# Query strips a head ahead, an older head's sums inside the key strip, norm roots read from PSUM, and a later start of two weight loads

## The chip, the cores and the metric

The kernel runs on one core of a Trainium2 chip, alone. The metric is device time in microseconds of that core, the median of several executions.

## What is computed

Two two-layer blocks, one after the other, on 256 latent tokens and 256 context tokens with 2048 features, everything in float32. The first block has a gated linear recurrence (layer 0) and a differential attention with 16 heads (layer 1), the second two layers (2 and 3) that join a gated spatial unit of 8 groups with grouped-query attention of 8 query heads on 2 key-value heads. Every layer starts with a modulated RMS norm and ends in an output projection with a gate and a residual. Cut to what the change touches:

```
def diff_attn_mixer(...):            # layer 1, per head
    q, k = rms_norm(q), rms_norm(k), rotated
    attn = softmax(q0 k0) - lam * softmax(q1 k1)
    o = rms_norm(attn @ v, subln_g) * (1 - lam_init)
    return (o * silu(g)) @ w_out
def second_block(...):               # layers 2 and 3
    h = rms_norm_2(x, norm_w) * (1 + scale) + shift
    u, v_sgu, za, q, k, v, zb = split(h @ w_in)
    q = rope(rms_norm_2(q, q_norm_w));  k = rope(rms_norm_2(k, k_norm_w))
    attn = softmax(q k_all * HEAD_DIM ** -0.5) @ v_all
    y = concat([sgu * silu(za), attn * silu(zb)]) @ w_out
```

Layer 3 is the last one: its queries and gates are wanted for the 256 latent tokens alone, in layer 2 for all 512.

## The kernel before

Activations lie feature-major: 16 tiles of 128 features by 512 tokens. Float32 products are made on TensorE (PE) in three reduced-precision products: high weights by high activations, high by low, low by high. A **strip** is a weight block of 2048 rows by 128 columns, 1 MB, in two halves of eight 128 by 128 tiles. Each strip goes the same way: SyncE loads a half into `raw` (`load_strip`, L215) once VectorE (DVE) has split what lay there before; ScalarE (ACT) copies it to a rounded high part (`split_hi`, L223), DVE subtracts that to get the low part (`split_lo`, L231), and PE runs 48 matmuls (`strip`, L249 to L251). There are two strip buffers. A strip's buffer is free for the next but one when its matmuls are done, so both splits wait for `strip_done`; ACT and DVE call `next_strip` right after it.

The order of all work is written out by hand: each engine runs its own list (`start_*`, `lru_*`, `att_*`, `sgu_*`, `kv_*`, `gqa_*`, `out_*`, `norm_*`) and waits on counting semaphores. Per-head work is a software pipeline: `body(j, par)` handles iteration i, in which head i is `here`, head i-1 `before` and head i-2 `older`. An engine never passes a waiting instruction of its own list.

- **Opening** (`start_*`). Eight groups of modulation weights of 4 MB each (four loads of 1 MB, POOL L1807, one buffer of four slots) feed products on PE (L299). SyncE holds the loads of strips 2 and 3 back until the products of six groups are done.
- **Norms of layers 1 to 3.** PE spreads the inverse root to all partitions in PSUM bank 6 (L493), ACT copies it to SBUF (L503), and DVE uses it in two products for each of 16 feature tiles (L541, L543); ACT and DVE make high and low parts of the result (L522, L550), and PE's first strips (L288) follow tile by tile.
- **Layer 1, per head** (`att_*`): key strip, scores, the ones-product that sums the squares of the older head's output (`sso`), query strip, the ones-product for the key (`ssk`, L1114), value strip, transposes, gate strip, weighted values. On ACT the four exponentials (L1174) stand ahead of the older head's square root (L1178), with a switch of the function table between them.
- **Layers 2 and 3, per head** (`gqa_*`): query strip of head i, its rotation of head i-1 (L1603), transposes of head i-2's weights (L1610, L1614), gate strip of head i, the ones-product for head i's query norm (L1622), weighted values of head i-2 (L1631, L1634), scores of head i-1 (L1645, L1648). ACT splits first and then copies and squares the query (L1688, L1689), which gives `q_evac`. The gate's bank goes through a tanh on ACT (L1706). Behind the last head the first two output strips (`out_first`, L625, L262) are interleaved with what is left of the pipeline, while ACT and DVE turn the 16 tiles of the mixer's output into high and low parts (`to_high`, `to_low`, L604, L609).

Of the kernel before, what the change touches and what calls it, by code (L numbers as in the profile page):

```python
# [83 lines left out]
def build(nc, ins, out):  # L84
    with ExitStack() as ctx:
# [444 lines left out]
        def norm_dve(dve, l):  # L530
# [5 lines left out]
            dve.wait_ge(S["rstd_done"], l + 1)  # L536
            dve.wait_ge(S["strip_done"], layer_strip[l])

            def context(k, c):
                dve.wait_ge(S["h_ready"], KT * l + k - 3)  # L540
                dve.scalar_tensor_tensor(out=hs4[c][:, 0:T], in0=xl[:, k, :], scalar=mod_a[:, bass.ds(k, 1), 0],  # L541
                                         in1=nb["rstd"][:, 0:T], op0=ALU.mult, op1=ALU.mult)
                dve.scalar_tensor_tensor(out=hs4[c][:, T:NT], in0=y[:, 1, k, :], scalar=mod_a[:, bass.ds(k, 1), 1],  # L543
                                         in1=nb["rstd"][:, T:NT], op0=ALU.mult, op1=ALU.mult).then_inc(S["hf_done"], 1)
# [529 lines left out]
        def att_pe(pe):  # L1074
            def body(j, par):
# [3 lines left out]
                def chunk(n):  # L1079
                    return lambda half: mod_chunk(pe, M_ATT + j, 2 * par + n) if half else None  # L1080
                first = isinstance(i, int) and i == 0
# [4 lines left out]
                elif here:  # L1086
                    ge(pe, A["v_evac"], i)
                    strip(pe, att_strip(j, par, 0), psum[:, K_BANK, :], NT, chunk(0))
# [13 lines left out]
                if older:  # L1102
                    pe.wait_ge(A["o_evac"], i - 1)
                    pe.matmul(psum[:, M_BANK, 0:T], ones, osq, start=True, stop=True).then_inc(A["sso"], 1)
# [49 lines left out]
        def att_act(act):  # L1154
            def body(j, par):
# [3 lines left out]
                if last:  # L1159
                    to_high(act, 1, 0, 6)  # L1160
                if here:
# [14 lines left out]
                if older:  # L1176
                    act.wait_ge(A["sso"], i - 1)
                    act.activation(osq, psum[:, M_BANK, 0:T], ACT.Sqrt, scale=1.0 / P, bias=eps_col).then_inc(A["sdo"], 1)  # L1178
# [402 lines left out]
        def gqa_strip(lay, j, par, c):  # L1581
            return Strip(S_NET2 + lay * L2_STRIPS + L2_ATT, 2 * par + c, j, 4)

        def gqa_pe(pe, lay):
            base, wide_ = HEADS2 * lay, lay == 0
            n = NT if wide_ else T
            def body(j, par):
                i = 2 * j + par
                here, before, older = live(i, HEADS2), live(i - 1, HEADS2), live(i - 2, HEADS2)
                last, end = (isinstance(i, int) and i == HEADS2 + n for n in range(2))  # L1590
                if last:
                    pe.wait_ge(B["q_evac"], base + HEADS2)
                    pe.wait_ge(B["sz"], base + HEADS2)
                    out_first(pe, 2 + lay, 0, 4)
                if end:
                    out_first(pe, 2 + lay, 10, 14)
                if here:
                    ge(pe, B["q_evac"], base + i)
                    strip(pe, gqa_strip(lay, j, par, 0), psum[:, 0, 0:n], n)
                if before:  # L1600
                    pe.wait_ge(B["qn"], base + i)
                    ge(pe, B["qt1"], base + i - 1)
                    pe.matmul(psum[:, 5, 0:T], rot2, q2[:, 0:T], start=True, stop=True).then_inc(B["rotq"], 1)  # L1603
                if last:
                    out_first(pe, 2 + lay, 4, 8)
                if older:
                    pe.wait_ge(B["attn"], base + i - 1)
                    for qt in range(2):
                        for kt in range(4):
                            mm = pe.transpose(psum[:, 2 + qt, kt * P:(kt + 1) * P], p2[qt][:, kt * P:(kt + 1) * P], ident)  # L1610
                    if wide_:
                        for qt in range(2):
                            for kt in range(2):
                                mm = pe.transpose(psum[:, 4, kt * T + qt * P:kt * T + (qt + 1) * P],  # L1614
                                                  p2[2][:, qt * T + kt * P:qt * T + (kt + 1) * P], ident)
                    mm.then_inc(B["attn_t"], 1)
                if here:
                    ge(pe, B["sz"], base + i)
                    strip(pe, gqa_strip(lay, j, par, 1), psum[:, 1, 0:n], n)
                    pe.wait_ge(B["q_evac"], base + i + 1)  # L1620
                    ge(pe, B["sdq"], base + i)
                    pe.matmul(psum[:, 6, 0:n], ones, q2s[:, 0:n], start=True, stop=True).then_inc(B["ssq"], 1)  # L1622
                if last:
                    out_first(pe, 2 + lay, 8, 10)
                if end:
                    out_first(pe, 2 + lay, 14, OUT_REST)
                if older:
                    pe.wait_ge(B["attn_sb"], base + i - 1)
                    ge(pe, B["y2"], base + i - 2)
                    for kt in range(4):  # L1630
                        mm = pe.matmul(psum[:, 7, 0:T], v2[par][:, kt * P:(kt + 1) * P], at2[:, kt, :], start=(kt == 0), stop=(kt == 3))  # L1631
                    if wide_:
                        for kt in range(2):
                            mm = pe.matmul(psum[:, 7, T:NT], v2[par][:, T + kt * P:T + (kt + 1) * P], at2c[:, kt, :],  # L1634
                                           start=(kt == 0), stop=(kt == 1))
                    mm.then_inc(B["av"], 1)
                if before:
                    if isinstance(i, int) and i == 1:
                        pe.wait_ge(B["kr"], 2 * (lay + 1))
                        pe.wait_ge(B["v_sb"], 2 * (lay + 1))  # L1640
                    pe.wait_ge(B["qr"], base + i)
                    ge(pe, B["attn_sb"], base + i - 1)
                    keys = k2[1 - par]
                    for qt in range(2):
                        mm = pe.matmul(psum[:, 2 + qt, :], q2r[:, qt * P:(qt + 1) * P], keys, start=True, stop=True)  # L1645
                    if wide_:
                        for qt in range(2):
                            mm = pe.matmul(psum[:, 4, qt * T:(qt + 1) * T], q2r[:, T + qt * P:T + (qt + 1) * P], keys[:, T:NT],  # L1648
                                           start=True, stop=True)
                    mm.then_inc(B["scores"], 1)  # L1650
            rounds(pe, body, HEADS2, 2, 4)

        def gqa_act(act, lay):
            base, wide_ = HEADS2 * lay, lay == 0
            n = NT if wide_ else T

            def body(j, par):
                i = 2 * j + par
                here, before, older = live(i, HEADS2), live(i - 1, HEADS2), live(i - 2, HEADS2)
                last, end = (isinstance(i, int) and i == HEADS2 + n for n in range(2))  # L1660
                if before:
                    act.wait_ge(B["ssq"], base + i)
                    act.activation(q2s[:, 0:n], psum[:, 6, 0:n], ACT.Sqrt, scale=1.0 / P, bias=eps_col).then_inc(B["sdq"], 1)
                if last:
                    to_high(act, 2 + lay, 0, 4)
                if older:
                    act.wait_ge(B["negmax"], base + i - 1)
                    ge(act, B["attn_t"], base + i - 2)
                    for qt in range(2):
                        ins_ = act.activation(p2[qt], psum[:, 2 + qt, :], ACT.Exp, scale=SCALE2, bias=nm2[:, qt:qt + 1],  # L1670
                                              accum_out=rs2[:, qt:qt + 1])
                    if wide_:
                        for qt in range(2):
                            ins_ = act.activation(p2[2][:, qt * T:(qt + 1) * T], psum[:, 4, qt * T:(qt + 1) * T], ACT.Exp, scale=SCALE2,
                                                  bias=nm2[:, 2 + qt:3 + qt], accum_out=rs2[:, 2 + qt:3 + qt])
                    ins_.then_inc(B["expd"], 1)
                if last:
                    to_high(act, 2 + lay, 4, 8)
                if end:
                    to_high(act, 2 + lay, 14, OUT_REST)  # L1680
                if here:
                    st = gqa_strip(lay, j, par, 0)
# [3 lines left out]
                    if isinstance(i, int) and i == 0:  # L1686
# [3 lines left out]
                if older:  # L1690
# [488 lines left out]
```

## Time and profile before

| | us |
|---|---|
| median of 3 executions | 2798.53 (2798.18 to 2805.46) |
| the profiled execution | 2805.79 |
| its span, first to last instruction | 2804.1 |
| PE busy in the span | 2639.0 (94%) |
| DVE busy | 2045.8 (73%) |
| ACT busy | 1224.6 (44%) |
| mean granted TensorE clock | 0.977 |

The profiled execution took 1.7 us more than its span and 7.3 us more than the median. PE is busy nearly everywhere, so the time is told by where PE stands idle and by where its clock is at the lower level. A PE row gives the start of a group of matmuls and its busy time; the next group starts some tenths before the busy time is over, since matmuls overlap. The number in square brackets is the idle time of the engine just before, with what ended it.

### The profile page before, as it was taken

The numbers are of one execution on the slowest core, as the hardware profiler recorded it, in microseconds if no ns is written. First come the engines' busy times: TensorE is split into PE (matmuls) and PEld (weight loads), VectorE is DVE, ScalarE is ACT, GpSimd is POOL, SyncE is SP. The second block draws the span as 40 slices with busy tenths as digits, with TensorE's granted clock in tenths as the row PEclk, the third lists the DMA queues.
The fourth block names the chain that finished last, engine by engine and source line by source line (L and its number), as shares of the span: only waits on it lengthen the run. The fifth ranks groups of instructions, "written<-read, shape, count | busy, mean of one in ns | idle before, by whom it ended". The sixth has DMA issues, their size and how long they took to land.

```text
span 2804.1 us, 39539 instructions
## 1 busy us (share of the span) xinstructions
PE 2639.0 (94%) x13490; PEld 2133.3 (76%) x13490; DVE 2045.8 (73%) x3196; ACT 1224.6 (44%) x1875; POOL 211.6 (8%) x402
## 2 busy tenths in 40 slices
PE   5799999999899999999989899999998997999989
PEld 1477777788677777777768788888886887998978
DVE  4399999999778788687877777764454666775655
ACT  3266556622443444444345433323444324544642
POOL 1110011011000000000000011100000100110000
PEclk8799999999999999999999899999999998999999
DMA  9765455476455565565655355532221643873325
GB/s 370 287 196 164 166 181 177 145 262 225 180 180 204 178 199 181 183 209 195 217 187 193 131 188 182 187 123 99 68 74 49 223 148 124 282 239 120 122 101 167
DMA packets 126557, 498.35 MB, mean 178 GB/s; under 512 B 14464, under 2 KB 16512, under 8 KB 116608
## 3 DMA queue, kind: packets, MB, share of 16 engines
q1 hardware_dynamic: 74176, 267.49, 27.7%
q0 software_dynamic: 52288, 229.66, 23.8%
q8 instruction: 53, 0.87, 0.1%
q14 instruction: 40, 0.33, 0.0%
HBM read 492.90 MB, written 4.19 MB: 177 GB/s over the span
## 4 chain that ended last, share of the span: by engine, by line
PE 75%; DVE 12%; issue 5%; DMA 4%; ACT 3%; DVEq 1%; POOL 0%; ACTq 0%; POOLq 0%; SPq 0%
PE psum L249 18%; PE psum L251 18%; PE psum L250 18%; PE psum L262 4%; DMA y<-in_mod_weights 2%; DVE w_lo L231 2%; PE psum L263 2%; DVE psum L409 2%; PE psum L299 2%; ACT w_hi L223 1%; PE psum L1631 1%; PE psum L1099 1%; PE psum L836 1%; DVE work L411 1%; PE psum L1645 1%
## 5 line engine op out<-in xcount | busy, mean ns | idle before, releaser
L249 PE MATMUL psum<-h_both,w_hi 128*128 128x512 f32 (+1 forms) x3264 | 1184.3, 363 | 5.6 <-DVE w_lo L231 5.6
L251 PE MATMUL psum<-h_both,w_lo 128*128 128x512 f32 (+1 forms) x3264 | 1156.1, 354 | 0.0
L250 PE MATMUL psum<-h_both,w_hi 128*128 128x512 f32 (+1 forms) x3264 | 1155.4, 354 | 0.0
L231 DVE TENSOR_TENSOR w_lo<-raw,w_hi 128x1024 fp32r<-128x1024 f32 x496 | 584.9, 1220 | 305.3 <-ACT w_hi L223 302.4
L249 PEld LDWEIGHTS psum<-h_both,w_hi 128*128 128x128 f32 x3264 | 619.6, 190 | 100.0 <-issue 13.2
L250 PEld LDWEIGHTS psum<-h_both,w_hi 128*128 128x128 f32 x3264 | 619.8, 190 | 92.4 <-issue 9.8
L251 PEld LDWEIGHTS psum<-h_both,w_lo 128*128 128x128 f32 x3264 | 619.1, 190 | 85.8
L223 ACT ACTIVATE w_hi<-raw 128x1024 fp32r<-128x1024 f32 x496 | 496.7, 1052 | 388.3 <-PE psum L251 301.4
L262 PE MATMUL psum<-h_both,w_hi 128*128 128x512 f32 x480 | 177.0, 409 | 10.0 <-DVE h_both L609 9.6
L263 PE MATMUL psum<-h_both,w_lo 128*128 128x256 f32 x480 | 137.0, 286 | 0.0
L409 DVE SCALAR_TENSOR_TENSOR psum<-y,modraw 128x1024 f32<-128x1024 f32 x98 | 120.3, 1228 | 21.1 <-DMA y<-in_mod_units 18.5
L411 DVE SCALAR_TENSOR_TENSOR y<-y,modraw 128x1024 f32<-128x1024 f32 x98 | 119.5, 1220 | 0.0
L262 PEld LDWEIGHTS psum<-h_both,w_hi 128*128 128x128 f32 x480 | 92.6, 193 | 34.2 <-issue 6.2
L263 PEld LDWEIGHTS psum<-h_both,w_lo 128*128 128x128 f32 x480 | 93.1, 194 | 1.5
L409 DVE SCALAR_TENSOR_TENSOR psum<-work,modraw 128x1024 f32<-128x1024 f32 x62 | 76.1, 1227 | 2.4 <-DMA work<-in_mod_units 2.4
L411 DVE SCALAR_TENSOR_TENSOR work<-work,modraw 128x1024 f32<-128x1024 f32 x62 | 75.6, 1220 | 0.0
L1165 ACT ACTIVATE y<-psum 128x512 f32<-128x512 f32 x16 | 9.6, 597 | 148.8 <-PE psum L251 146.8
L288 PE MATMUL psum<-h_both,w_hi 128*128 128x512 f32 (+1 forms) x128 | 54.9, 429 | 20.6 <-DVE h_both L550 16.8
L1191 ACT ACTIVATE y<-psum 128x512 f32<-128x512 f32 x16 | 9.6, 597 | 143.6 <-PE psum L251 143.6
L299 PE MATMUL psum<-modraw,cond 128*32 128x512 f32 x384 | 60.0, 711 | 12.2 <-DMA modraw<-in_mod_weights 8.6
L836 PE MATMUL psum<-work 128*128 128x512 f32 x128 | 59.0, 604 | 6.9 <-DVE work L931 6.6
L757 DVE SCALAR_TENSOR_TENSOR y<-psum,mod,work 128x256 f32<-128x256 f32 x32 | 15.4, 483 | 67.0 <-PE psum L251 57.8
(289 smaller groups left out, 3127.3 us busy)
## 6 DMA issues: line engine op xcount, KB each, us to landing
raw<-in_weights SPq DMA_DIRECT2D x496, 512.0 KB, 4.4
y<-in_mod_units POOLq DMA_DIRECT2D x130, 512.0 KB, 4.2
modraw<-in_mod_weights POOLq DMA_DIRECT2D x48, 1024.0 KB, 5.5
work<-in_mod_units POOLq DMA_DIRECT2D x62, 512.0 KB, 4.6
y<-in_mod_weights POOLq DMA_DIRECT2D x16, 1024.0 KB, 9.1
xl<-in_mod_units POOLq DMA_DIRECT2D x32, 512.0 KB, 4.8
modraw<-in_mod_units POOLq DMA_DIRECT2D x32, 512.0 KB, 4.7
modraw<-in_cond_rows POOLq DMA_DIRECT2D x6, 1024.0 KB, 8.0
```

The lines of the kernel that those rows point to most:

```text
L223: act.activation(w_hi[:, par, half, :], raw[:, 2 * par + half, :], ACT.Copy).then_inc(S["split_hi"], 1)
L231: dve.tensor_tensor(w_lo[:, par, half, :], raw[:, 2 * par + half, :], w_hi[:, par, half, :].bitcast(F32), ALU.subtract).then_inc(S["split_ ...
L249: pe.matmul(dst, hi, h_hi[:, k, 0:n], start=(k == 0), stop=False)
L250: pe.matmul(dst, hi, h_lo[:, k, 0:n], start=False, stop=False)
L251: mm = pe.matmul(dst, lo, h_hi[:, k, 0:n], start=False, stop=(k == KT - 1))
L262: pe.matmul(joined, hi, h_both[:, :, k, 0:T], start=(k == 0), stop=False)
L263: return pe.matmul(bank[:, 0:T], lo, h_hi[:, k, 0:T], start=False, stop=False)
L288: pe.matmul(dst, hi, h_hi[:, k, 0:n], start=(k == 0), stop=False)
L299: mm = pe.matmul(bank[32 * j:32 * j + 32, :], cond[:, 4 * q + j, :], chunk[:, j, :], start=(q == 0), stop=(q == 3))
L409: dve.scalar_tensor_tensor(out=out, in0=mw[:, half, :], scalar=0.5, in1=rows[:, 0, part], op0=ALU.mult, op1=ALU.mult, accum_out=macc[:, pa ...
L411: dve.scalar_tensor_tensor(out=mw[:, half, :], in0=mw[:, half, :], scalar=0.5, in1=rows[:, 1, part], op0=ALU.mult, op1=ALU.mult, accum_out ...
L836: pe.matmul(psum[:, GATE_BANK + g, :], lw["gw"][par][:, g, :], lw["xc"], start=True, stop=True).then_inc(L["gate_done"], 1)
```

## The change

Four edits. **(A)** In layers 2 and 3 the query strip of head i now runs in the same iteration as the gate strip of head i-1; the strips lie in memory in that new order, and the pipeline is one iteration deep instead of two. On PE an iteration is: query strip i, transposes of head i-1, ones-product of head i, gate strip i-1, rotation i, weighted values i-1, scores i. ACT and DVE follow: exponentials first, gate last. The first two iterations and the last are written out with an order of their own; `out_first` now starts behind the last gate strip, and waits for that gate. **(B)** In layer 1 the older head's ones-product moves between the two halves of the key strip, and its square root on ACT in front of the key's copies, followed by a one-element Exp. **(C)** The norms of layers 1 to 3 read the inverse root from PSUM; ACT's copy is gone there. **(D)** Strips 2 and 3 are loaded after the products of seven groups.

```
@@ norm_sqrt / norm_dve
-            act.wait_ge(S["rstd_ps"], l + 1)
-            act.activation(nb["rstd"], psum[:, SS_BANK, :], ACT.Copy).then_inc(S["rstd_done"], 1)
+            else:
+                act.wait_ge(S["rstd_ps"], 1)
+                act.activation(nb["rstd"], psum[:, SS_BANK, :], ACT.Copy).then_inc(S["rstd_done"], 1)
-                                         in1=nb["rstd"][:, 0:T], op0=ALU.mult, op1=ALU.mult)
+                                         in1=psum[:, SS_BANK, 0:T], op0=ALU.mult, op1=ALU.mult)
@@ att_pe / att_act
+                def sums():
+                    pe.wait_ge(A["o_evac"], i - 1)
+                    pe.wait_ge(A["sdq"], min(i, HEADS1) if isinstance(i, int) else i)
+                    pe.matmul(psum[:, M_BANK, 0:T], ones, osq, start=True, stop=True).then_inc(A["sso"], 1)
+                def key_strip(half):
+                    if half:
+                        mod_chunk(pe, M_ATT + j, 2 * par)
+                    elif older:
+                        sums()
+                if older and here:
+                    root()
+                    act.activation(warm, eps_col, ACT.Exp)
@@ gqa_pe
+                if here:
+                    ge(pe, B["q_evac"], base + i)
+                    strip(pe, q_strip(lay, j, par), psum[:, 0, 0:n], n, (lambda half: None if half else turned(0)) if second else None)
+                if second:
+                    scores(0, 0)
+                if before and not second and not end:
+                    turned_weights(i - 1)
+                if here:
+                    sums(i)
+                if before:
+                    ge(pe, B["sz"], base + i - 1)
+                    strip(pe, z_strip(lay, j, par), psum[:, 1, 0:n], n)
+                if second or end:
+                    turned_weights(i - 1)
+                if end:
+                    out_first(pe, 2 + lay, 0, 4)
+                if here and not first:
+                    turned(i)
+                if before:
+                    weighted(i - 1, 1 - par)
+                if here and not first:
+                    scores(i, par)
+                if end:
+                    out_first(pe, 2 + lay, 4, OUT_REST)
@@ gqa_act
+                if here:
+                    st = q_strip(lay, j, par)
+                    act.wait_ge(S["strip_done"], st.s + 1)
+                    next_strip(split_hi, act, st)
+                    ge(act, B["qr"], base + i)
+                    act.activation(q2[:, 0:n], psum[:, 0, 0:n], ACT.Copy)
+                    act.activation(q2s[:, 0:n], psum[:, 0, 0:n], ACT.Square).then_inc(B["q_evac"], 1)
@@ sync
-            sp.wait_ge(S["mod_used"], 4 * (MOD_FIRST - 2))
+            sp.wait_ge(S["mod_used"], 4 * (MOD_FIRST - 1))
```

PE in the steady heads of layer 3, before: the query strip ends (L251), rotation, transposes, gate strip (its first rows), and, behind it, ones-product, weighted values, scores.

```order
L1603 MATMUL psum<-modraw,consts 128x256 [waits gqa_qt1,gqa_qn]
L1610 MATMUL psum<-consts,work 128x128 [waits gqa_attn]
L1610 MATMUL psum<-consts,work 128x128 x7
L243 ISA [waits gqa_sz]
L249 MATMUL psum<-h_both,w_hi 128x256 [waits split_lo]
...
L1622 MATMUL psum<-modraw,consts 128x256 [waits gqa_sdq,gqa_q_evac]
L1631 MATMUL psum<-work,modraw 128x256 [waits gqa_y2,gqa_attn_sb]
L1631 MATMUL psum<-work,modraw 128x256 x3
L1645 MATMUL psum<-modraw 128x512 [waits gqa_attn_sb,gqa_qr]
```

The same place now, again from the end of a query strip.

```order
L1641 MATMUL psum<-consts,work 128x128 [waits gqa_attn]
L1641 MATMUL psum<-consts,work 128x128 x7
L1635 MATMUL psum<-modraw,consts 128x256 [waits gqa_sdq,gqa_q_evac]
L243 ISA [waits gqa_sz]
L249 MATMUL psum<-h_both,w_hi 128x256 [waits split_lo]
...
L1615 MATMUL psum<-modraw,consts 128x256 [waits gqa_qt1,gqa_qn]
L1653 MATMUL psum<-work,modraw 128x256 [waits gqa_y2,gqa_attn_sb]
L1653 MATMUL psum<-work,modraw 128x256 x3
L1625 MATMUL psum<-modraw 128x512 [waits gqa_attn_sb,gqa_qr]
```

The ones-product (L1622, now L1635), which waits for the query's copy and square (`q_evac`), stood behind the gate strip and now stands ahead of it, with the transposes alone between the query strip and it; the rotation went behind the gate strip.

ACT in the same heads now, from the split at the end of a query strip.

```order
L223 ACTIVATE w_hi<-raw 128x1024 [waits strip_done,raw_in2]
L223 ACTIVATE w_hi<-raw 128x1024 [waits raw_in3]
L1735 ACTIVATE modraw<-psum 128x256 [waits gqa_qr]
L1736 ACTIVATE modraw<-psum 128x256
L1712 ACTIVATE work<-psum 128x4x128 [waits gqa_av,gqa_attn_t]
L1712 ACTIVATE work<-psum 128x4x128
L1743 ACT_TABLE_LOAD
L1743 ACTIVATE modraw<-psum,small 128x256 [waits gqa_ssq]
```

As before, the two halves of the split (L223) stand ahead of the query's copy and square (L1688 and L1689, now L1735 and L1736).

ACT in the heads of layer 1 now, from the older head's root on.

```order
L1175 ACT_TABLE_LOAD
L1175 ACTIVATE work<-psum,small 128x256 [waits att_sso]
L1178 ACT_TABLE_LOAD
L1178 ACTIVATE small<-small 128x1
L1183 ACTIVATE y<-psum 128x512 [waits att_kr,strip_done]
L1184 ACTIVATE y<-psum 128x512
L223 ACTIVATE w_hi<-raw 128x1024 [waits strip_done,raw_in0]
L223 ACTIVATE w_hi<-raw 128x1024 [waits raw_in1]
L1192 ACTIVATE y,small<-psum,small 128x512 [waits att_negmax,att_attn_t]
```

The root (L1178 before, L1175 now) stood behind four exponentials and now stands ahead of the key's copies; a head has two table switches more.

## Rows read from the trace of the kernel before

**Rows 1.** Page: busy time by engine, granted clock by fortieths of the span
```profile
PE 2639.0 (94%) x13490; PEld 2133.3 (76%) x13490; DVE 2045.8 (73%) x3196; ACT 1224.6 (44%) x1875; POOL 211.6 (8%) x402
PEclk8799999999999999999999899999999998999999
```

**Rows 2.** PE's waits in layer 1's heads: us in total, times, longest
```profile
PE psum L1114 <- issue: 18.6, 14, 1.4
```

**Rows 3.** Timeline of one head of layer 1: start, busy, engine
```profile
1146.91 1.10 PE L1114 MATMUL psum<-y,consts 128*128 128x512 f32 x2 [1.34 <-issue]
...
1145.05 1.28 ACT L1178 ACT_TABLE_LOAD   x1
1146.34 0.47 ACT L1178 ACTIVATE work<-psum,small 128x256 f32<-128x256 f32 x1
...
1182.23 0.60 ACT L1165 ACTIVATE y<-psum 128x512 f32<-128x512 f32 x1 [9.31 <-PE psum L251]
```

**Rows 4.** Timeline of a steady head of layer 3, PE then ACT
```profile
2625.41 0.59 PE L1603 MATMUL psum<-modraw,consts 128*128 128x256 f32 x2
2626.14 1.09 PE L1610 MATMUL psum<-consts,work 128*128 128x128 f32 x8
2626.99 0.36 PE L249 MATMUL psum<-h_both,w_hi 128*128 128x256 f32 x1
...
2625.78 2.01 ACT L223 ACTIVATE w_hi<-raw 128x1024 fp32r<-128x1024 f32 x2 [0.81 <-PE psum L251]
...
2630.77 0.38 ACT L1689 ACTIVATE modraw<-psum 128x256 f32<-128x256 f32 x1
```

**Rows 5.** Timeline of a steady head of layer 2, PE then ACT
```profile
2045.67 0.59 PE L1603 MATMUL psum<-modraw,consts 128*128 128x256 f32 x2
2046.10 1.04 PE L1610 MATMUL psum<-consts,work 128*128 128x128 f32 x8
2047.33 0.48 PE L249 MATMUL psum<-h_both,w_hi 128*128 128x512 f32 x1
...
2046.03 2.01 ACT L223 ACTIVATE w_hi<-raw 128x1024 fp32r<-128x1024 f32 x2 [6.52 <-PE psum L251]
2051.22 0.59 ACT L1689 ACTIVATE modraw<-psum 128x512 f32<-128x512 f32 x1
```

**Rows 6.** PE's waits around layer 3's heads, the largest of six
```profile
PE psum L262 <- DVE h_both L609: 7.0, 3, 3.1
```

**Rows 7.** PE's waits around layer 2's heads, the largest of four
```profile
PE psum L625 <- DVE h_both L609: 12.1, 5, 3.0
```

**Rows 8.** PE after stalls of 1.8 to 2.3 us
```profile
2574.77 0.70 PE L1603 MATMUL psum<-modraw,consts 128*128 128x256 f32 x2 [1.79 <-DVE modraw L1741]
2455.92 0.68 PE L1393 MATMUL psum<-work 128*128 128x128 f32 x4 [2.27 <-DVE work L1493]
2710.12 0.50 PE L262 MATMUL psum<-h_both,w_hi 128*128 128x512 f32 x1 [1.85 <-DVE h_both L609]
```

**Rows 9.** Stretches behind them: us, busy by engine, PEclk, DMA share, GB/s
```profile
2576.00:2578.00 2.00, 2.00 (x12) 2.00 (x11) 1.97 (x4) 0.00 (x0) 0.00 (x0) 0.54 0.46 125
2456.50:2460.00 3.50, 3.50 (x19) 3.50 (x19) 3.00 (x6) 1.91 (x3) 0.53 (x1) 0.53 0.71 208
2712.00:2714.00 2.00, 1.44 (x10) 1.13 (x10) 0.68 (x2) 0.47 (x1) 0.00 (x0) 1.00 0.00 0
1126.00:1171.00 45.00, 42.98 (x249) 34.52 (x247) 34.20 (x49) 19.99 (x36) 1.58 (x3) 1.00 0.45 164
```

**Rows 10.** Timeline of layer 2's norm: root spread, copied, used
```profile
1559.35 0.60 ACT L503 ACTIVATE work<-psum 128x512 f32<-128x512 f32 x1 [1.43 <-PE psum L493]
1560.24 0.48 DVE L541 SCALAR_TENSOR_TENSOR work<-xl,small,work 128x256 f32<-128x256 f32 x1 [1.07 <-ACT work L503]
1553.31 0.48 DVE L760 SCALAR_TENSOR_TENSOR xl<-psum,mod,xl 128x256 f32<-128x256 f32 x1 [1.38 <-PE psum L265]
```

**Rows 11.** A stretch of the opening: busy by engine, PEclk, DMA share, GB/s
```profile
94.00:96.00 2.00, 2.00 (x14) 1.78 (x14) 0.17 (x1) 0.60 (x1) 0.53 (x1) 1.00 1.00 422
```

More of the change, by code:

```diff
@@ L1101, in body @@
                         mm.then_inc(A["scores"], 1)
-                if older:
-                    pe.wait_ge(A["o_evac"], i - 1)
-                    pe.matmul(psum[:, M_BANK, 0:T], ones, osq, start=True, stop=True).then_inc(A["sso"], 1)
+                if older and not here:
+                    sums()
                 if here:
@@ L1175, in body @@
                                            accum_out=rs1[:, n:n + 1]).then_inc(A["expd"], 1)
[L1176 to L1178 removed]
+                if older and not here:
+                    root()
                 if here:
@@ L1587, in body @@
             def body(j, par):
                 i = 2 * j + par
-                here, before, older = live(i, HEADS2), live(i - 1, HEADS2), live(i - 2, HEADS2)
-                last, end = (isinstance(i, int) and i == HEADS2 + n for n in range(2))
-                if last:
+                here, before = live(i, HEADS2), live(i - 1, HEADS2)
+                first, second, end = (isinstance(i, int) and i == m for m in (0, 1, HEADS2))
+                if here:
+                    ge(pe, B["q_evac"], base + i)
+                    strip(pe, q_strip(lay, j, par), psum[:, 0, 0:n], n, (lambda half: None if half else turned(0)) if second else None)
@@ L1617, in body @@
[L1617 to L1626, printed above, removed]
@@ L1637, in body @@
[L1637 to L1650, printed above, removed]
@@ L1657, in body, with gate @@
+            def gate(h, par):
+                ge(act, B["y2"], base + h - 1)
+                act.activation(sz3[par][:, 0:n], psum[:, 1, 0:n], ACT.Tanh, scale=0.5).then_inc(B["tz"], 1)
             def body(j, par):
                 i = 2 * j + par
[L1659 to L1680, printed above, removed]
+                here, before = live(i, HEADS2), live(i - 1, HEADS2)
+                first, second, end = (isinstance(i, int) and i == m for m in (0, 1, HEADS2))
+                if before and not second:
+                    exps(i - 1)
                 if here:
-                    st = gqa_strip(lay, j, par, 0)
+                    st = q_strip(lay, j, par)
@@ L1781, in body @@
-                if here:
-                    dve.wait_ge(B["tz"], base + i + 1)
-                    dve.scalar_tensor_tensor(out=sz3[par][:, 0:n], in0=sz3[par][:, 0:n], scalar=1.0, in1=psum[:, 1, 0:n],
-                                             op0=ALU.add, op1=ALU.mult).then_inc(B["sz"], 1)
-            rounds(dve, body, HEADS2, 2)
+                here, before = live(i, HEADS2), live(i - 1, HEADS2)
+                first, second, end = (isinstance(i, int) and i == m for m in (0, 1, HEADS2))
```

290 lines of the change are left out of this document (174 added, 116 removed).

## The prediction

> **What bounds the kernel now.** I read the page first. PE is busy for 2639.0 of 2804.1 us and its clock digit is 9 in most fortieths [rows 1], so there is little to take: a gain must come out of PE's idle time or out of stretches at the lower of its two clock levels, and anything that makes PE wait in a dense stretch is paid in full. Next come PE's waits, for each stretch that the change touches, since the last wait there is what an edit removes or puts in its place. In layer 1 one line holds nearly all: the key's ones-product L1114 stood idle 18.6 us, 14 times [rows 2]. In layer 3 PE's waits around the heads sum to 12.9 us in six rows of that view, in layer 2 to 13.8 us in four; the largest of each [rows 6, 7] lies behind the last head, where output tiles are turned into high and low parts. Last, the timelines of one steady head in each of these layers [rows 3 to 5]. In layer 2 the heads have no idle time on PE, in layer 3 0.2 to 0.3 us a head.
>
> **Edit B, the older head's sums (layer 1).** L1114 waits for the older head's root. That stands on ACT behind four exponentials: a table switch of 1.28 us from 1145.05, then 0.47 us, done at 1146.81, and PE starts at 1146.91 after 1.34 us idle [rows 3]. The change computes this root in the middle of the next key strip. ACT sat idle for 9.31 us there, until the key strip's end at 1182.23 [rows 3], and half of that, 4.7 us, holds two switches (2.56), the root (0.47) and the one-element Exp. PE's matmuls are the same, in another place. The key's own root now needs a switch of 1.28 us too, but its taker, DVE, no longer waits for the older root before it scales the weights, and so comes to it earlier as well. So the wait goes, 14 times: **-18.6 us**. Bounds: nothing, if the next wait takes its place, and a little over 18.6 with the small waits behind it. I take the full value, because the other things that L1114 waits for (the key's copy, the query root of the head before) are done during the strips.
>
> **Edit A, steady heads.** The ones-product of the query norm waits for `q_evac`, ACT's copy and square of the query strip. It used to stand behind the gate strip, so nobody noticed how late this comes. In layer 3 the query strip's last matmul issues just before 2625.41; ACT's split starts at 2625.78 and takes 2.01 us; then copy and square, 0.38 us each and 0.66 together; a handover of 0.05 more [rows 4]. That is 0.37 + 1.95 + 0.66 + 0.05 = 3.03 us. Between the query strip and the ones-product PE now has only the transposes, 2626.14 to 2626.99 = 0.85 us. PE therefore stalls **2.2 us in each such head**. In layer 2: 0.36 + 1.95 + 1.08 + 0.05 = 3.44 us, less transposes of 2046.10 to 2047.33 = 1.23 us, again 2.2 us [rows 5]. Heads 2 to 7 of both layers run so: 12 x 2.2 = **+26.4 us**. Behind the waiting product nothing else can run on PE; the gate strip is queued there with its weights ready. What the new order wins in the steady heads is the 0.3 and less between rotation (0.43 us long) and transposes [rows 4]: -1.1 us over five heads. Softmax is covered: its chain has the whole query strip to run in, and loses its table switch to the gate's tanh, which is not waited for.
>
> **Edit A, first and last heads.** With nothing but the query strip ahead of it the first ones-product waits 3.0 us in layer 3 and 3.4 in layer 2; the second has the scores ahead of it (1.7 and 2.4 us) and waits 1.3 and 1.0; two rotations of layer 3 wait 0.7 each for the norm. Head 0's weighted values wait for ACT's copy of its transposes, which stands behind the split (2.0), a table switch (1.28), the tanh and itself: 2.9 and 4.0 us. At the end `out_first` waits for the last gate, which on ACT stands behind two half splits, three output tiles, and the copy of the transposes: 4.8 and 6.0 us. Then PE finds its tiles ready. These are estimates from the durations of [rows 4, 5] (a half strip, scores and copies scaled from them). Sum: 13.4 us in layer 3 and 14.4 in layer 2, against 12.9 and 13.8 of now: **+1.1 us**.
>
> **Edit A, the clock.** PE's clock is granted at two levels, 1.2 and 2.4 GHz. After a stall of 1.79 us and one of 2.27 us [rows 8] the granted clock stood at 0.54 and 0.53 [rows 9]; the second of these stretches lasted 3.5 us, so it lost 3.5 x (1 - 0.53) = 1.6 us. After one of 1.85 us it did not fall, and in layer 1 no stall of 1.34 us brought it down [rows 8, 9]. A stall of 2.2 us in a dense stretch will thus often cost 1.6 to 1.7 us more, and the transposes ahead of it are light work. I take three stalls in four: 12 x 0.75 x 1.7 = **+15.3 us**; the bounds are 0 and 12 x 1.7 = 20.4. The stretches at the ends have such falls now and will have about as many. The Trainium skill ("TensorE: Matmul & The Clock Gate", "Why this matters for your kernels") asks for no idle gaps above some 3 us between bursts, by which stalls of 2.2 us would pass unpunished and the sum would lack this term. The rows speak against it.
>
> **Edit C, the norms.** In layer 2 ACT's copy of the root starts at 1559.35 and DVE's first product at 1560.24, after 1.07 us idle [rows 10]. Without the copy DVE starts about 0.8 us sooner. In layers 1 and 3 DVE is busy with a split for most of that time, so I take 0.4 and 0.2. The 96 products now read one operand from PSUM; a product of the same form with an operand there takes 0.48 us, as the one from SBUF does [rows 10]. **-1.4 us**; the bounds are 0 and -2.7 (three times 0.9).
>
> **Edit D, the opening.** The DMA engines are full when the two strips (2.1 MB) are fetched [rows 11], so moving them behind one more group frees the queue for that group and loads the next: the bytes before PE's last opening product stay nearly the same. I take **0**. The bounds are those 2.1 MB at 422 GB/s, 5 us, saved or, if PE's last group gets the crowd, lost.
>
> **Sum.** -18.6 + 26.4 - 1.1 + 1.1 + 15.3 - 1.4 + 0 = +21.7 us, from the profiled 2805.8 to 2827.5 us. That execution was 7.3 us above the median; on the median of 2798.5 the sum gives **2820 us**.
>
> **Rivals.**
> (1) *The clock does not fall* behind the new stalls. For it: the 1.85 us stall. Against: the two others. 2820.2 - 15.3 = 2805 us, within 0.3%.
> (2) *It falls behind every one*, and once or twice more at the ends: +5 to +9, some 2827 us.
> (3) *Faster.* The ones-product of the query norm hardly waits, because ACT delivers `q_evac` sooner than my chain says. It decides at the stall of a steady head: all else sums to -20.0, so with stall and clock together under 1.0 us a head the kernel is faster by over 8 us. With 0.5 us and no fall it is 2798.5 - 20.0 + 6 = 2784 us. For it: ACT is idle when each of these strips ends [rows 4, 5], so nothing else delays it. Against: on ACT the split stands ahead of the copy, in the rows of the order and in the trace [rows 4, 5], and it can't start before the strip ends.
> (4) *Edit B does not do what it says*: with two more table switches a head on ACT the key's root or the copies come late, and half the 18.6 comes back: 2829 us.
>
> **How the numbers follow.** 0.3% is 8.4 us, about what a measurement can tell from no change: 2790 to 2807. Forecast 0.56, (1) 0.15, (2) 0.16, (3) 0.07, (4) 0.06. Faster comes from (3) alone, 0.07. The same is (1) and a thin edge of the forecast, less a part of (1) that ends above: 0.15. Slower 0.78. The range leaves out (3) and the upper part of (4), and runs from below (1), where some stalls are also shorter, to (2) with its margin for edit D: 2800 to 2831.
>
> **What would show it.** In the profile after: no idle time ahead of layer 1's key product; L1635 as a new line in PE's waits, with 14 to 16 waits, 12 of them near 2.2 us, some 35 us in all, released by ACT's square; a period of a steady head that is about 2 us longer in layer 3 and 2.2 us longer in layer 2, without a fall of the clock; fallen clock in most of the stretches behind these stalls; ACT's L503 once instead of four times. The prediction is wrong if L1635 doesn't wait, if the clock stays at the upper level through the heads of layers 2 and 3, or if a wait of layer 1 takes the place of L1114's.

## The result, and the profile after

| | before | after |
|---|---|---|
| median of 13 runs each, side by side | 2805.46 us (2795.78 to 2810.28) | 2811.06 us (2808.25 to 2820.99) |
| ratio | 1 | 1.0028, 95% interval 1.0018 to 1.0037 |
| profiled execution, span | 2804.1 us | 2809.4 us |
| mean granted clock | 0.977 | 0.972 |

The ratio, times the 2805.4 us of before, makes the cost of the change 7.9 us (5.0 to 10.4), about 0.3%. (It goes by the means of the runs; the two medians differ by 5.6 us.) That is slower, the way that was forecast, by a little over a third of the 21.7 us forecast. It is also less than the 8.4 us up to which the prediction calls a result the same; the 13 runs of each kernel tell it from nothing all the same, since the interval leaves out 1. On the page the busy times hardly move, and nothing on it names a cause; compare with [rows 1].

```profile
PE 2642.3 (94%) x13490; PEld 2139.0 (76%) x13490; DVE 2049.0 (73%) x3196; ACT 1256.7 (45%) x1910; POOL 211.8 (8%) x402
PEclk7799999999999999999999999999999999999999
```

A small difference can be the sum of two large ones, so the next view is PE's waits (us in all, times, longest). These rows are those in the code that changed.

```profile
PE psum L1635 <- ACT modraw L1736: 29.8, 16, 3.1
PE psum L626 <- DVE work L1810: 5.8, 1, 5.8
PE psum L262 <- DVE work L1810: 4.5, 1, 4.5
PE psum L1653 <- ACT work L1715: 3.8, 1, 3.8
PE psum L1653 <- ACT work L1712: 2.8, 1, 2.8
PE psum L1615 <- DVE modraw L1797: 0.5, 1, 0.5
```

The key's ones-product (L1114 before [rows 2], now L1125) has no row: 18.6 us of waiting are gone. In its place stands L1635, the ones-product of the query norm, which now waits in every head of layers 2 and 3, released by ACT's square. The waits of [rows 6, 7] on DVE's high and low parts have given way to one long wait a layer on the last gate (5.8 and 4.5 us).

Layer 1, the end of a key strip in the timeline of ACT, then of PE (start, busy):

```profile
1160.81 1.28 ACT L1175 ACT_TABLE_LOAD   x1
1165.03 0.47 ACT L1175 ACTIVATE work<-psum,small 128x256 f32<-128x256 f32 x1 [2.94 <-PE psum L1086]
1165.52 1.28 ACT L1178 ACT_TABLE_LOAD   x1
1166.82 0.20 ACT L1178 ACTIVATE small<-small 128x1 f32<-128x1 f32 x1
```
```profile
1171.40 1.99 PE L1111 MATMUL psum<-y,work 64*128 64x512 f32 x8
1179.17 1.02 PE L1125 MATMUL psum<-y,consts 128*128 128x512 f32 x2
```

The older head's root and both table switches now lie in what was ACT's idle time before the key's copies, 9.31 us in the head of [rows 3], and no idle time is printed ahead of L1125. A head of layer 1 takes 42.43 or 44.29 us where it took 43.97 or 45.8.

A steady head of layer 3, PE then ACT, to be held against [rows 4]:

```profile
2646.32 0.29 PE L251 MATMUL psum<-h_both,w_lo 128*128 128x256 f32 x1
2646.44 1.04 PE L1641 MATMUL psum<-consts,work 128*128 128x128 f32 x8
2649.32 0.70 PE L1635 MATMUL psum<-modraw,consts 128*128 128x256 f32 x2 [1.85 <-ACT modraw L1736]
```
```profile
2646.72 2.00 ACT L223 ACTIVATE w_hi<-raw 128x1024 fp32r<-128x1024 f32 x2 [1.92 <-PE psum L251]
2648.63 0.36 ACT L1735 ACTIVATE modraw<-psum 128x256 f32<-128x256 f32 x1
2648.90 0.37 ACT L1736 ACTIVATE modraw<-psum 128x256 f32<-128x256 f32 x1
```

From the start of the last matmul of the query strip (2646.32) to the ones-product (2649.32) it is 3.00 us, of which ACT spends 1.91 on splitting weights while PE waits for the copy and the square behind them. PE has its transposes to fill 1.15 us of that and stands for 1.85.

The granted clock behind four of the twelve steady stalls, in windows of 2 us (columns as in [rows 9]); the stalls end at 1944.36, 2007.82, 2589.89 and 2608.68:

```profile
1946.00:1948.00 2.00, 2.00 (x10) 1.65 (x9) 0.20 (x1) 1.76 (x2) 0.00 (x0) 1.00 0.86 332
2009.50:2011.50 2.00, 2.00 (x7) 1.52 (x6) 0.24 (x1) 1.71 (x2) 0.00 (x0) 0.50 0.98 340
2591.50:2593.50 2.00, 2.00 (x19) 2.00 (x18) 0.87 (x1) 1.08 (x2) 0.00 (x0) 1.00 0.87 315
2610.50:2612.50 2.00, 2.00 (x11) 2.00 (x10) 1.08 (x1) 0.88 (x2) 0.00 (x0) 0.50 0.85 303
```

In layer 3's rows PE has 11 matmuls in 2 us at 0.50 where it has 19 at 1.00. The clock stays down for about 3.5 us each time, some 1.7 us by half the clock. It fell behind 5 of the 12 (those that end at 2007.82, 2072.88, 2608.68, 2629.04 and 2686.98), with stalls of 1.83 to 1.92 us in both groups. What a fall costs in time is read from two heads of layer 3 with the same 120 matmuls, from one L1635 to the next, first without a fall, then with one:

```profile
2649.32:2668.19 18.87, 16.95 (x120) 15.45 (x121) 11.52 (x17) 10.40 (x17) 0.00 (x0) 1.00 0.35 111
2608.68:2629.04 20.36, 18.44 (x120) 16.94 (x120) 11.35 (x17) 10.39 (x17) 0.00 (x0) 0.92 0.33 104
```

The head is 1.5 us longer; the layer 2 head behind 2007.82 takes 33.27 us where its neighbours take 31.69 and 31.77, 1.5 to 1.6 us more.

By layer, each taken from its norm's first L493 to that of the next: layer 1 takes 21.5 us less, layer 2 14.0 more, layer 3 and the end 12.4 more.

### The profile page after: what moved, and what is told of

Its sections match the earlier page's. It is cut to its first block, busy times and chain, and to the rows that moved or that the text cites. A ratio compares the mean times of both kernels' runs of the same rounds, so it can differ in the third digit from the quotient of the medians.

```text
span 2809.4 us, 39594 instructions
## 1 busy us (share of the span) xinstructions
PE 2642.3 (94%) x13490; PEld 2139.0 (76%) x13490; DVE 2049.0 (73%) x3196; ACT 1256.7 (45%) x1910; POOL 211.8 (8%) x402
## 3 DMA queue, kind: packets, MB, share of 16 engines
q0 software_dynamic: 52288, 229.66, 23.9%
## 4 chain that ended last, share of the span: by engine, by line
PE 73%; DVE 12%; issue 5%; DMA 4%; ACT 4%; DVEq 1%; POOL 0%; ACTq 0%; POOLq 0%; SPq 0%
PE psum L249 18%; PE psum L251 18%; PE psum L250 18%; PE psum L262 4%; DVE psum L409 2%; PE psum L263 2%; DMA y<-in_mod_weights 2%; DVE w_lo L231 2%; ACT w_hi L223 2%; PE psum L299 2%; PE psum L1111 1%; DMA work<-in_mod_units 1%; PE psum L1653 1%; DVE work L411 1%; DVE h_both L551 1%
## 5 line engine op out<-in xcount | busy, mean ns | idle before, releaser
L251 PE MATMUL psum<-h_both,w_lo 128*128 128x512 f32 (+1 forms) x3264 | 1161.1, 356 | 0.0
L223 ACT ACTIVATE w_hi<-raw 128x1024 fp32r<-128x1024 f32 x496 | 496.9, 1052 | 466.5 <-PE psum L251 367.7
L251 PEld LDWEIGHTS psum<-h_both,w_lo 128*128 128x128 f32 x3264 | 622.2, 191 | 85.9
L1790 DVE RECIPROCAL modraw<-modraw 128x512 f32<-128x512 f32 (+1 forms) x16 | 40.9, 2553 | 32.3 <-ACT modraw L1743 32.3
L1208 ACT ACTIVATE y<-psum 128x512 f32<-128x512 f32 x16 | 9.6, 597 | 116.9 <-PE psum L251 116.9
```

The source lines that it names most:

```text
L223: act.activation(w_hi[:, par, half, :], raw[:, 2 * par + half, :], ACT.Copy).then_inc(S["split_hi"], 1)
L251: mm = pe.matmul(dst, lo, h_hi[:, k, 0:n], start=False, stop=(k == KT - 1))
```

## The experiments

**Each edit alone.** Theory one: the time is the sum of the forecast's terms, each in the place where the prediction put it, and only sizes are wrong. Its rival: the small total hides another mechanism (an edit that does something else, or edits that only act together). Four kernels make one edit each. In short, what of the change stays in each:

```diff
 A: -             + [c for h in heads for c in (q + h, zb + h)])
    +             + [q + heads[0]] + [c for n in range(1, HEADS2) for c in (q + heads[n], zb + heads[n - 1])] + [zb + heads[-1]])
 B: +                if older and here:
    +                    root()
    +                    act.activation(warm, eps_col, ACT.Exp)
 C: -            dve.wait_ge(S["rstd_done"], l + 1)
    +            dve.wait_ge(S["rstd_ps"], l + 1)
 D: -            sp.wait_ge(S["mod_used"], 4 * (MOD_FIRST - 2))
    +            sp.wait_ge(S["mod_used"], 4 * (MOD_FIRST - 1))
```

> Edit A alone (the new order of the heads in layers 2 and 3). Theory 1, each term of the forecast had its place right and its size wrong: the 12 steady heads lose some 2.0 us each and the clock falls at about 5 of them, so A alone costs 24 + 8 - 2 at the ends = +30 us (ratio about 1.011), with L1635-type waits of 28 to 31 us in 16 waits. Theory 2, the forecast's price of A is right (+41.7 us, ratio 1.015) and edits C and D give back some 12 us that were not foreseen.

> Edit B alone (older head's sums in the key strip of layer 1). Theory 1: -21.5 us (1.54 us in each of 14 heads; ratio about 0.992), nothing idle ahead of the key's ones-product. Theory 2: -18.6 us. Rival: below half of it, if the two table switches come through; then a wait of ACT or DVE stands ahead of the key product.

> Edit C alone (norm products read the root from PSUM). Theory 1: -1.4 to -2 us, below what can be told from nothing (ratio 0.9993). Theory 2: -5 us or more.

> Edit D alone (strips 2 and 3 loaded after the products of seven groups). Theory 1: 0 within 2 us either way; the last opening group's product starts at the same time within 2 us. Theory 2: -5 us, the whole price of 2.1 MB taken out of the opening.

| edit alone | ratio (95%) | us |
|---|---|---|
| A | 1.0104 (1.0089 to 1.0119) | +29.2 |
| B | 0.9922 (0.9907 to 0.9936) | -21.9 |
| C | 0.9993 (0.9984 to 1.0003) | -2.0 |
| D | 0.9999 (0.9987 to 1.0010) | -0.3 |

The microseconds are the ratio less 1, times the 2805.4 us of before. The four ratios multiply to 1.0017; the change as a whole has 1.0028. The edits add up within the intervals, so no interaction is seen, though one of a few us could hide in them: theory one stands. A alone costs 29.2 us and not the 41.7 of the forecast, and C and D together give back 2.3, not 12. In the kernel with A alone, PE's waits hold the new wait and the old one side by side:

```profile
PE psum L1618 <- ACT modraw L1719: 29.8, 16, 3.1
PE psum L1114 <- issue: 18.6, 14, 1.4
```

Here the clock fell behind only 3 of the 12 steady stalls, which are as long as in the changed kernel (1.84 to 1.92 us); about 5 had been expected.

**Edit A left out.** B, C and D together, the heads of layers 2 and 3 as they were.

> Edits B, C and D with the heads of layers 2 and 3 as before. Theory 1: the parts add up, -21.9 - 2 - 0.3 = -24 us, ratio 0.9914. Rival: parts overlap or disturb each other and the ratio lies off the product of the single ones by more than 0.002.

Measured: 0.9913 (0.9898 to 0.9928), so -24.4 us. On top of these A costs 1.0028 / 0.9913, or 1.0116, some 32 us; alone it cost 29.2, the same within the intervals.

**The stall taken away.** If A's cost is the stall of L1635 with what the clock adds, it should vanish when ACT copies and squares the strip before it splits the next weights:

```diff
                     act.wait_ge(S["strip_done"], st.s + 1)
-                    next_strip(split_hi, act, st)
                     ge(act, B["qr"], base + i)
...
                     act.activation(q2s[:, 0:n], psum[:, 0, 0:n], ACT.Square).then_inc(B["q_evac"], 1)
+                    next_strip(split_hi, act, st)
```

> The change with one thing more: in the heads of layers 2 and 3 ACT copies and squares the query strip ahead of both halves of the split, not behind them. Theory 1 (the two half splits ahead of the copy are the stall): q_evac comes 1.95 us sooner, the waits of the ones-product fall from 29.8 us to under 5, no clock falls are left in the steady heads, and the kernel wins 23 + 8 + some 4 in the first heads = 35 us: ratio to the kernel before about 0.990. Rival (the ones-product only shows a wait that something behind it would have anyway, as the weights of the next strip or DVE's chain): the wait moves to the gate strip or to the rotation, and less than 10 us are won.

Measured: 0.9916 (0.9902 to 0.9930), 2785.45 us. That is 31 us below the change, where 35 were expected, and the rival's "less than 10" is out. The clock falls in none of the steady heads. In its trace a steady head of layer 3 reads, on ACT:

```profile
2627.14 0.38 ACT L1734 ACTIVATE modraw<-psum 128x256 f32<-128x256 f32 x1 [2.24 <-PE psum L251]
2627.42 0.38 ACT L1735 ACTIVATE modraw<-psum 128x256 f32<-128x256 f32 x1
2627.69 2.01 ACT L223 ACTIVATE w_hi<-raw 128x1024 fp32r<-128x1024 f32 x2
```

and in PE's waits L1635 is left with the first heads of the two layers; the rotation behind the gate strip, which nothing covers now, takes a part over (7.9 us, where the changed kernel had 0.5):

```profile
PE psum L1615 <- DVE modraw L1797: 7.9, 9, 2.0
PE psum L1635 <- ACT modraw L1735: 1.9, 2, 1.2
```

With the stall gone edit A is worth nothing either way, within the intervals of some 4 us: 0.9916 with it, 0.9913 without. So its cost came from the place of two instructions of 0.4 to 0.6 us on ACT.

**The stall halved.** One half split stays ahead of the copy, the other goes behind it. The stalls of the steady heads are then 0.89 to 0.98 us, as here:

```profile
2643.69 0.70 PE L1635 MATMUL psum<-modraw,consts 128*128 128x256 f32 x2 [0.90 <-ACT modraw L1736]
```

```diff
-                    next_strip(split_hi, act, st)
+                    split_hi(act, st.pair + 1, st.par, halves=(0,))
...
                     act.activation(q2s[:, 0:n], psum[:, 0, 0:n], ACT.Square).then_inc(B["q_evac"], 1)
+                    split_hi(act, st.pair + 1, st.par, halves=(1,))
```

> As e5, but one half split stays ahead of the copy. Theory 1: the stall is about 0.9 us in place of 1.85, that is 12 us less in the steady heads. Clock, first theory (only stalls well above 1.3 us bring it down): no fall in the steady heads, another 8 us less; about 22 us below the change, ratio to before about 0.995. Clock, second theory (falls come in proportion to the idle time): 2 to 3 falls are left, about 17 us below the change.

Measured: 0.9954 (0.9940 to 0.9968), -12.9 us, 10.7 us more than with the copy first. By the two traces a steady head of layer 2 is 1.06 us longer than with the copy first. One of layer 3 is only 0.28 longer, since the rotation's wait of 0.53 us goes there when the ones-product waits. With 2.0 us in the first heads that is 10 us, so next to nothing is left for the clock, and in the trace it doesn't fall behind any of the twelve stalls (a row of this kernel stands under the next experiment, which goes the other way).

**The stall made longer.** ACT's copy and square are cut into eight pieces each; the work is the same.

```diff
-                    act.activation(q2[:, 0:n], psum[:, 0, 0:n], ACT.Copy)
-                    act.activation(q2s[:, 0:n], psum[:, 0, 0:n], ACT.Square).then_inc(B["q_evac"], 1)
+                    for a in range(0, n, n // 8):
+                        act.activation(q2[:, a:a + n // 8], psum[:, 0, a:a + n // 8], ACT.Copy)
+                    for a in range(0, n, n // 8):
+                        ins_ = act.activation(q2s[:, a:a + n // 8], psum[:, 0, a:a + n // 8], ACT.Square)
+                    ins_.then_inc(B["q_evac"], 1)
```

> The changed kernel with ACT's copy and its square of each query strip cut into eight pieces each: 14 more instructions ahead of the release of the ones-product, in all 16 heads. A piece should cost 0.07 (what is left of the time between the starts of two such instructions when the columns go to nothing, from 0.28 us at 256 columns and 0.49 at 512) to 0.2 us, so the stalls of the steady heads grow from 1.85 us to some 2.8 (2.8 to 4.5), by 1.0 us a head or more; the work is the same. The question is what decides whether the clock falls, which it did behind 5 of 12 such stalls. Theory one (a longer stall is met by the chip's look at the activity more surely): it falls behind nearly all 12, 7 x 1.7 = 12 us beside the 16 x 1.0 = 16 us of waiting; +28 us on the changed kernel's 1.003, ratio about 1.013, and about 0.004 more for each microsecond that a stall grows beyond that less 0.6. Theory two (it falls for a reason other than the length, such as where in the program the stall lies): still 4 to 6 of 12, and the time grows by the stalls alone, 16 us, ratio about 1.0085.

Measured: 1.0125 (1.0100 to 1.0149), theory one's 1.013 and outside theory two's 1.0085. The stalls of the steady heads are 2.70 to 2.79 us, a growth of 0.9:

```profile
2681.40 1.22 PE L1635 MATMUL psum<-modraw,consts 128*128 128x256 f32 x2 [2.71 <-ACT modraw L1738]
```

The same 792 matmuls of layer 2's heads 2 to 7 in three kernels, first the one with the halved stall, then the changed kernel, then this one (windows; after the busy times PEclk, DMA share, GB/s):

```profile
1950.00:2135.00 185.00, 179.19 (x792) 143.22 (x792) 91.45 (x122) 76.25 (x127) 0.00 (x0) 1.00 0.22 69
```
```profile
1944.00:2137.00 193.00, 182.35 (x792) 145.72 (x792) 90.10 (x120) 75.36 (x126) 0.00 (x0) 0.98 0.20 66
```
```profile
1954.00:2159.00 205.00, 190.15 (x792) 150.72 (x792) 89.28 (x119) 79.65 (x197) 0.00 (x0) 0.94 0.19 62
```

The clock went 1.00, 0.98, 0.94 and PE's busy time 179.2, 182.4, 190.2 us for equal work. Of this kernel's windows behind layer 3's stalls the first is the one exception (clock 1.00), the second has the clock at 0.50, as it is at some point behind the other ten stalls of both layers:

```profile
2642.00:2644.00 2.00, 2.00 (x19) 2.00 (x18) 0.77 (x1) 1.19 (x2) 0.00 (x0) 1.00 0.89 317
2661.50:2663.50 2.00, 2.00 (x11) 2.00 (x11) 0.54 (x1) 1.42 (x2) 0.00 (x0) 0.50 0.86 301
```

| stall of a steady head | falls of the clock | seen in |
|---|---|---|
| 0.89 to 0.98 us | 0 of 12 | stall halved |
| 1.28 to 1.36 us | 0 of 14 | before, layer 1 |
| 1.83 to 1.92 us | 8 of 24 | after 5 of 12, A alone 3 of 12 |
| 2.70 to 2.79 us | 11 of 12 | stall longer |

Two limits of this table. Its second row is of other code, layer 1. And each count is from one execution of a kernel: the six executions with the longer stall took 2829 to 2849 us at mean clocks of 0.973 to 0.962, and the traced one is the slowest of them, so 11 of 12 is the high end of what this kernel does. Its ratio, from all six, still leaves theory two out. Outside the steady heads the counts are few and mixed: behind the 3.14 us stall of layer 2's first head the clock fell in the changed kernel and not with A alone, and behind the 2.72 us stall of layer 3's first head it fell in neither.

**Further than both kernels.** The copy goes first, as above, and at the end of layers 2 and 3 the last gate is taken on ACT and DVE before the splits and high and low parts that stood ahead of it:

```diff
+                        gate(i - 1, 1 - par)
+                        to_high(act, 2 + lay, 0, 1)
                         split_hi(act, st.pair + 1, st.par, halves=(0,))
-                        to_high(act, 2 + lay, 0, 1)
+                        to_high(act, 2 + lay, 1, 4)
+                        weights(i - 1)
                         split_hi(act, st.pair + 1, st.par, halves=(1,))
...
```

> As e5, and behind the last gate strip ACT and DVE treat the gate first, then the first output tile, then the half splits. Expected by theory 1: PE's wait behind the last transposes falls from 5.8 to about 2.5 us in layer 2 and from 4.5 to about 2.5 in layer 3, 5 us below e5, ratio to before about 0.988. Rival: later tiles come too late and the wait returns further on, nothing won.

Measured: 0.9885 (0.9869 to 0.9901), 2775.04 us, 9 us below the version with the copy first, where 5 were expected. The one long wait a layer is gone; what is left in its place is a wait of 2.3 us a layer for low parts of weights. Then ACT copies head 0's transposes before it splits:

```diff
                     act.wait_ge(S["strip_done"], st.s + 1)
+                    if second:
+                        weights(0)
...
-                if second:
-                    weights(0)
```

> The version that beat both kernels, with one thing more: in the second iteration of layers 2 and 3, ACT copies head 0's transposes (weights(0)) as soon as the gate strip is done, ahead of its split, the table switch and the tanh. In the best version so far PE waits 3.81 us there in layer 2 (1919.86) and 1.56 in layer 3 (2553.70), 5.4 us in all, behind 2.01 + 1.28 + 0.6 us of ACT's work. Theory one (ACT's order alone makes this wait): the copies are done 0.5 to 1.7 us after the transposes, so some 0.6 to 1.2 us of wait is left, 4 us go, and up to two falls of the clock (1.7 each) with them: ratio 0.985 to 0.987 where the version without it had 0.9885. Rival (the wait passes to DVE's gate or to the low parts of the next strip, which then come 1 to 2 us later): ratio 0.988 to 0.989 as without it, with a new wait of 2 to 3 us at L249 or L1625.

Measured: 0.9886 (0.9864 to 0.9907). The wait at L1653 shrank as theory one says (3.8 and 1.6 us to 1.3 and none), and no new wait of 2 to 3 us appeared, but the ratio is the rival's and not theory one's 0.985 to 0.987. Its interval reaches both. So both versions ran once more, side by side:

> The earlier best version once more, beside its successor on the same chip: ratio 0.9885 as before, 0.987 to 0.990.

> The version with head 0's transposes copied first, beside the version without it on the same chip; in different sessions they gave 0.9886 (0.9864 to 0.9907) and 0.9885. Theory one (the 4.1 us of PE's waits that went from the trace, 3.81 and 1.56 to 1.29 and none, are 4.1 us of time): its ratio is 0.0015 to 0.002 under that of the version without it. Rival (they come back later): the two ratios agree within 0.0007.

Measured: 0.9878 (0.9861 to 0.9894) and 0.9855 (0.9838 to 0.9873), medians 2772.79 and 2766.80 us. PE's waits at this line, in the first of them and in the second:

```profile
PE psum L1653 <- ACT work L1715: 3.8, 1, 3.8
...
PE psum L1653 <- ACT work L1712: 1.6, 1, 1.6
```
```profile
PE psum L1653 <- ACT work L1715: 1.3, 1, 1.3
```

4.1 us of waiting went; the ratios differ by 0.0023 and the medians by 6 us. That is theory one's side, though the two intervals overlap and the first measurement did not show it, so this last step is likely and not shown. The last version is the fastest of the study, 40 us under before.

## Why the prediction came out as it did

The sign, the mechanisms and their places were right. The effect was forecast almost three times too large. Every term came out below its forecast (C and D by less than can be told from nothing), and the clock's alone makes half of the difference. Part of the closeness of the time itself is luck: the forecast of 2820 us starts from a median of 2798.5 us of three executions, while 13 gave 2805.5. The change came to 2811, 9 us under the forecast, but from the prediction's own start the measured cost gives 2806.4 us, 14 under it.

- **Edit B**: forecast -18.6, the profile has -21.5 (14 heads at 1.54) and the edit alone -21.9. The prediction had named "a little over 18.6" as a bound and took the idle time alone. The 1.34 us is idle time by the ends of pipelined matmuls; a head became shorter by 0.20 us more than that. I read this as the overlap that neighbouring matmuls have when nothing separates them; no run tests it by itself.
- **Edit A, steady heads**: forecast 26.4 - 1.1 = 25.3. Heads take turns between two lengths some 0.1 us apart. Without a fall of the clock, those of layer 3 take 18.87 and 18.79 us where they took 17.04 and 16.88 (+1.87 on the mean), those of layer 2 31.69 and 31.77 where they took 29.61 (+2.12): 6 x 1.87 + 6 x 2.12 = 23.9. The stall itself was put too high, 2.2 us for 1.85. The prediction counts from the end of the strip, where the next matmul starts; from there (2646.44) the ones-product starts after 2.88 us where 3.03 were forecast, and the transposes cover 1.03 us of it, not 0.85. In the sum this nearly cancels, since a head grew by more than its smaller stall (in layer 2 by 0.26 us more), which the forecast had not counted.
- **First and last heads**: forecast 13.4 + 14.4 = 27.8 against 26.7 before, +1.1; measured 12.4 + 13.3 = 25.7 (layer 3: 2.72 + 1.00 + 0.50 + 2.78 + 0.53 + 4.47 + 0.39; layer 2: 3.14 + 0.56 + 3.81 + 5.77), -1.0. The large waits were where the prediction put them. Overstated were the rotations of layer 3 (1.4 us for 0.5) and the two waits for the last gate (4.8 and 6.0 us for 4.47 and 5.77); layer 2's second ones-product was to wait 1.0 us and waited 0.56.
- **The clock**: forecast 12 x 0.75 x 1.7 = 15.3; measured five falls at 1.5 us, 7.5. This is the largest miss, and the term that made the forecast too large. "I take three stalls in four" rested on three stalls, two of which were followed by a fall. Over 24 such stalls the share is one in three, and "fallen clock in most of the stretches", which the prediction named as a sign, did not come. The size of a fall was nearly right. The stall of 2.2 us was also not the stall of the trace, which is 1.85 us, and between 1.34 us (none) and 2.7 (11 of 12 in one execution) the share climbs, so a third of a microsecond may matter. By the Trainium skill ("TensorE: Matmul & The Clock Gate", "Why this matters for your kernels"), which wants no idle gaps above some 3 us between bursts, no stall of these steady heads would have brought the clock down; the traces do not agree, with 19 falls behind 36 stalls of 1.83 to 2.79 us. At the first and last heads of layers 2 and 3 the prediction took the falls as equal, and they nearly are: PE was busy at the lower clock for 17.1 us there before and for 15.7 after.
- **Edit C**: forecast -1.4, alone -2.0 (-4.5 to +0.8). In layer 2 DVE now stands idle for 0.44 us before its first product, released by PE's spreading of the root, where it stood for 1.07 us behind ACT's copy [rows 10], so 0.63 us went where 0.8 were forecast. With its operand in PSUM the product takes the same 0.48 us:

```profile
1538.43 0.48 DVE L542 SCALAR_TENSOR_TENSOR work<-xl,small,psum 128x256 f32<-128x256 f32 x1 [0.44 <-PE psum L493]
```

- **Edit D**: forecast 0, alone -0.3 (-3.6 to +2.8).

The terms as measured: -21.5 + 23.9 - 1.0 + 7.5 - 2.0 - 0.3 = +6.6 us. The two profiled executions differ by 5.3 in span, all runs by 7.9 (5.0 to 10.4). The last two terms are from ratios whose intervals are wider than the terms.

Of the rivals, (1) without a fall of the clock and (2) with one behind every stall were two ends of one thing: at 1.85 us it is neither, and the longer stall shows nearly (2) at work, the halved one (1). The total of rival (1), +6.4 us, is closer to the measured one than the forecast's, and its condition is false all the same: the clock fell five times, and the terms of edit B, of the steady heads and of the ends made room for that. The total alone would have chosen the wrong one. Rival (3), ACT delivering sooner, was not what this kernel does, but it is what the version with the copy first makes it do: the prediction gave it 14.5 us under before with stalls of 0.5 us left; with none left in those heads the version is 23.6 us under before. Rival (4) is out, by edit B alone.

## What to carry to other kernels

When work is moved ahead on the engine that is the bound, look at what the waited-for engine does first when the moved step ends: here a 1.9 us split stood ahead of the copy and square (0.7 us in layer 3, 1.1 in layer 2) that PE waited for, and swapping the two turned a change that costs 8 us into one that gains 24. A total near zero may be two large effects, and an edit at a time separates them cheaply. A stall on a busy TensorE has two prices, its own length and the chance that the clock falls behind it (here 1.5 us a fall); take the chance from as many stalls of that length as the traces have, not from three.

## What was not expected of the hardware

The fall of the clock isn't a matter of yes or no at one length of a stall. In the same steady code, behind stalls equal to 0.1 us, it fell in 5 of 12 heads in one kernel and 3 of 12 in another; it never fell behind 26 stalls of 0.89 to 1.36 us, and in one execution fell behind 11 of 12 steady stalls of 2.70 to 2.79 us. Twice of those it stayed low for 7 us instead of 3.5. What else than the length decides a single case at 1.85 us these runs don't show.
